# The memory stage of a two-block network rebuilt: who splits the weights, where norms, squares and products stand, and norm weights applied inside the split

## The reference, cut to what matters

```python
mem_n = rms_norm(mem, mem_norm_g)                      # 256 x 2048
h = rms_norm(x, norm_g[0])                             # 512 x 2048
proj = h @ dn_w_in                                     # decay/beta, delta net, cross attention, gates
kv = mem_n @ w_kv                                      # 256 x 2048: 4 heads, keys and values of 256
k = rms_norm(kv[..., :1024] by head, kn_g); v = kv[..., 1024:]
...                                                    # delta net (12 pairs of heads), cross attention
x = x + (concat(mix, xa) * silu(z)) @ w_out            # mix is 3072 wide, xa 1024
```

## Time and profile before

| | us |
|---|---|
| median of 3 runs | 3722.05 (3721.0 to 3726.62) |
| profiled execution | 3725.82 |
| its span | 3724.0 |
| TensorE busy in it | 3395.2 (91%) |
| VectorE, ScalarE, GpSimd busy | 1524.5, 841.8, 1786.0 |
| mean granted TensorE clock | 0.969 |

### The profile page before, as it was taken

One profiled execution on the slowest core, in us unless ns is written; L12 is line 12 of the kernel. 1 busy time (PEld: TensorE's weight loads), 2 busy tenths in 40 slices (PEclk: granted clock), 3 DMA queues, 4 the chain that ended last, 5 costly groups with the idle time before them and its releaser, 6 DMA issues.

```text
span 3724.0 us, 47370 instructions
## 1 busy us (share of the span) xinstructions
PE 3395.2 (91%) x17232; PEld 2797.9 (75%) x17232; DVE 1524.5 (41%) x2077; ACT 841.8 (23%) x1269; POOL 1786.0 (48%) x1828
## 2 busy tenths in 40 slices
PE   7699989999999999999979998999988888879897
PEld 6667777887788778877768786777767777658685
DVE  2442234444444443444342213344345555541523
ACT  4322123223322332233220101111122222210111
POOL 4545544234433443334315675666654544436574
PEclk9899999999999999999989999999999999999998
DMA  5212221111111111111124223222221112232122
GB/s 207 102 63 85 91 74 57 51 60 70 68 39 64 65 68 51 56 62 68 59 94 152 86 101 124 97 84 91 96 96 59 64 68 70 90 113 101 68 99 81
DMA packets 53364, 306.69 MB, mean 82 GB/s; under 512 B 5012, under 2 KB 7188, under 8 KB 21812
## 3 DMA queue, kind: packets, MB, share of 16 engines
q1 hardware_dynamic: 33984, 247.48, 19.1%
q10 hardware_dynamic: 19316, 58.32, 4.2%
HBM read 284.74 MB, written 21.04 MB: 82 GB/s over the span
## 4 chain that ended last, share of the span: by engine, by line
PE 73%; DVE 14%; ACT 6%; issue 5%; POOL 1%; DMA 1%; ACTq 0%; DVEq 0%; POOLq 0%; SPq 0%
PE gemm_ps L388 18%; PE gemm_ps L390 18%; PE gemm_ps L389 18%; DVE arena L774 9%; ACT arena L1417 3%; DVE arena L780 3%; PE bankC L517 3%; PE bankA L505 3%; PE bankB L515 2%; PE bankA L674 1%; POOL w_lo L346 1%; ACT L1417 1%; DVE a_lo L774 1%; PE bankB L562 1%; PE bankB L563 1%
## 5 line engine op out<-in xcount | busy, mean ns | idle before, releaser
L388 PE MATMUL gemm_ps<-a_hi,w_hi 128*128 128x512 f32 (+1 forms) x3744 | 1516.8, 405 | 116.0 <-DVE a_lo L774 83.3
L390 PE MATMUL gemm_ps<-a_hi,w_lo 128*128 128x512 f32 (+1 forms) x3744 | 1451.8, 388 | 0.0
L389 PE MATMUL gemm_ps<-a_lo,w_hi 128*128 128x512 f32 (+1 forms) x3744 | 1449.8, 387 | 0.0
L361 POOL CAST w_hi<-w_raw 128x512 fp32r<-128x512 f32 x880 | 544.6, 661 | 1825.3 <-issue 1819.3
L346 POOL TENSOR_TENSOR w_lo<-w_raw,w_hi 128x512 fp32r<-128x512 f32 x944 | 1249.5, 1354 | 70.1 <-ACT w_hi L1417 70.1
L388 PEld LDWEIGHTS gemm_ps<-a_hi,w_hi 128*128 128x128 f32 x3744 | 718.1, 192 | 283.0 <-DVE a_lo L774 72.3
L390 PEld LDWEIGHTS gemm_ps<-a_hi,w_lo 128*128 128x128 f32 x3744 | 716.3, 191 | 143.8
L389 PEld LDWEIGHTS gemm_ps<-a_lo,w_hi 128*128 128x128 f32 x3744 | 719.1, 192 | 127.8 <-issue 9.6
L774 DVE TENSOR_TENSOR arena<-gemm_ps,arena 128x512 f32<-128x512 f32 (+3 forms) x145 | 96.0, 662 | 803.2 <-PE gemm_ps L390 798.7
L774 DVE RECIPROCAL arena<-arena 128x512 f32<-128x512 f32 (+2 forms) x70 | 172.7, 2468 | 361.8 <-ACT arena L1417 359.9
L1417 ACT ACTIVATE arena<-arena 128x512 f32<-128x512 f32 (+5 forms) x334 | 204.4, 612 | 437.2 <-DVE arena L774 423.3
(11 more groups left out here) (151 smaller groups left out, 2225.5 us busy)
## 6 DMA issues: line engine op xcount, KB each, us to landing
w_raw<-w_stream SPq DMA_DIRECT2D x236, 1024.0 KB, 4.8
y_scratch<-arena ACTq DMA_DIRECT2D x20, 512.0 KB, 3.5
arena<-y_scratch ACTq DMA_DIRECT2D x15, 512.0 KB, 3.6
arena<-gc_scratch ACTq DMA_DIRECT2D x12, 512.0 KB, 3.6
arena<-x_t ACTq DMA_DIRECT2D x1, 4096.0 KB, 13.3
arena<-y_scratch ACTq DMA_DIRECT2D x1, 4096.0 KB, 25.5
x_scratch<-arena ACTq DMA_DIRECT2D x1, 4096.0 KB, 13.2
y_out<-arena ACTq DMA_DIRECT2D x4, 1024.0 KB, 3.9
```

What stands on the lines that cost most here:

```text
L361: pool.tensor_copy(part(w_hi, w, q), part(w_raw, w, q)).then_inc(pool_step, 1)
L388: pe.matmul(o, hi, a_hi[:, k, 0:width], start=(k == 0), stop=False)
L389: pe.matmul(o, hi, a_lo[:, k, 0:width], start=False, stop=False)
L390: last = pe.matmul(o, lo, a_hi[:, k, 0:width], start=False, stop=(k == KT - 1))
```

## The change

The memory stage: half of memT, the gains and the first constants come before the second weight tile and the rest, and x follows in two halves. The weight of the memory's norm is applied by ScalarE's copy into `a_hi` (its scale) and by one VectorE instruction that multiplies and subtracts into `a_lo`. Six sums of squares stand ahead of the first tile's matmuls and ten between them. VectorE makes both parts of tiles 0 and 1 and the low part of tiles 2 to 17 (one instruction of 2048 elements), ScalarE the high part of tiles 2 to 17; GpSimd starts with tile 18. Squares of x, their sums, x's root and the products of x (in place), the key norms and v's transposes stand between the tiles. Fills 4 and 7 apply the norm weight in the two parts of the split. In the last pair of heads three buffers hold y, and four blocks are split ahead of the steps. The core of the diff (cut lines of the old order are described above; engines in the order SyncE, GpSimd, TensorE, VectorE, ScalarE):

```diff
 EARLY = 6
-X_FROM = 7
+AHEAD = 4
+SELF_CUT = W_AB + 2
+X_SQUARES = {4: 0, 5: 4, 7: 8, 8: 12}
+X_PRODUCTS = {9: (0, 4), 10: (4, 8), 12: (8, 12), 14: (12, 14), 15: (14, 16)}
...
-            for w in range(2):
-                sp.dma_start(w_raw[:, w, :, :], weights[w]).then_inc(raw_loaded[w], 16)
+            sp.dma_start(w_raw[:, 0, :, :], weights[0]).then_inc(raw_loaded[0], 16)
+            sp.wait_ge(s["mem_in"], 16)
+            sp.dma_start(w_raw[:, 1, :, :], weights[1]).then_inc(raw_loaded[1], 16)
...
-            with pool.Fori(0, W_AB // 2) as i:
+            with pool.Fori(0, (W_END - SELF_CUT) // 2) as i:
                 for w in range(2):
-                    low_tile(w, i)
-            with pool.Fori(0, (W_END - W_AB) // 2) as i:
-                for w in range(2):
-                    cut_tile(w, i + W_AB // 2, i)
+                    cut_tile(w, i + SELF_CUT // 2, i)
...
+            pe.wait_ge(s["par_loaded"], 32)
+            for k in range(6):
+                memory_sum(k)
             for c in range(W_AB):
                 for k in range(KT):
                     gemm(W_MEM, c, k, 0 if c == 0 else None, width=M)
+                    if c == 0 and k + 6 < KT:
+                        memory_sum(k + 6)
+                if c % 2 == 1 and 3 <= c < 3 + 2 * XH:
+                    if c == 3:
+                        pe.wait_ge(s["root_ready"], 1)
+                    kv_sums((c - 3) // 2)
+                if c == 8:
+                    pe.wait_ge(s["x_acc"], KT)
+                    pe.matmul(bankC[:, 1, :], ones, root, start=True, stop=True).then_inc(s["sq_summed"], 1)
+                if c >= 10:
+                    if c == 14:
+                        pe.wait_ge(s["root_ready"], 2)
+                    v_transposes(c - 10)
+            for c in (6, 7):
+                v_transposes(c)
...
                 for k in range(blocks):
+                    v.wait_ge(act_hi, CUT_AT[f] + k + 1)
                     if gain is not None:
-                        for kk in ((0, 1, 2) if k == 0 else (k + 2,)):
-                            if kk < KT:
-                                product(kk)
-                    v.wait_ge(act_hi, CUT_AT[f] + k + 1)
+                        op(v.scalar_tensor_tensor, a_lo[:, k, 0:width], src[:, k, :], gains(gain + k),
+                           a_hi[:, k, 0:width].bitcast(F32), ALU.mult, ALU.subtract,
+                           sem=act_lo, value=CUT_AT[f] + k + 1)
+                        continue
                     op(v.tensor_tensor, a_lo[:, k, 0:width],
-                       stage[:, k % 4, 0:width] if gain is not None else src[:, k, :],
+                       src[:, k, :],
...
+            v.wait_ge(s["par_loaded"], 32)
+            def low_tile(t):
+                w, n = tile_at(W_MEM, t)
+                if t < 2:
+                    v.wait_ge(raw_loaded[w], 16)
+                    op(v.tensor_copy, w_hi[:, w, :, :], w_raw[:, w, :, :])
+                else:
+                    v.wait_ge(s[f"mem_hi{w}"], n)
+                op(v.tensor_tensor, w_lo[:, w, :, :], w_raw[:, w, :, :], w_hi[:, w, :, :].bitcast(F32), ALU.subtract,
+                   sem=cut[w], value=n + 1)
+            for k in range(KT):
+                v.wait_ge(act_hi, k + 1)
+                op(v.scalar_tensor_tensor, a_lo[:, k, 0:M], src_mem[:, k, :], gains(C_MEMN + k),
+                   a_hi[:, k, 0:M].bitcast(F32), ALU.mult, ALU.subtract, sem=act_lo, value=k + 1)
+                if k in (1, 9):
+                    low_tile(k // 9)
             reciprocal_root(0, M)
             for c in range(W_AB):
                 scaled(kv[:, c, :], W_MEM, c, width=M)
+                if c + 2 < SELF_CUT - 1:
+                    low_tile(c + 2)
+                if c + 2 in X_SQUARES:
+                    for k in range(X_SQUARES[c + 2], X_SQUARES[c + 2] + 4):
                         v.wait_ge(s["squared"], KT + k + 1)
                         if k == 0:
...
+                if c in KV_NORM:
+                    h = KV_NORM[c]
+                    v.wait_ge(s["kv_root"], h + 1)
+                    op(v.reciprocal, stage[:, h, 0:M], stage[:, h, 0:M])
+                    for e in range(2):
+                        op(v.scalar_tensor_tensor, kv[:, 2 * h + e, :], kv[:, 2 * h + e, :], gains(C_XK + e),
+                           stage[:, h, 0:M], ALU.mult, ALU.mult, sem=s["kv_norm"] if e else None, value=h + 1)
+                if c == 8:
+                    v.wait_ge(s["root_ready"], 2)
+                    op(v.reciprocal, root, root, sem=s["rstd_ready"], value=2)
+                if c in X_PRODUCTS:
+                    for k in range(*X_PRODUCTS[c]):
+                        op(v.scalar_tensor_tensor, src0[:, k, :], src0[:, k, :], gains(C_NORM + k), root,
+                           ALU.mult, ALU.mult, sem=s["x_made"], value=k + 1)
+            fill(1, src0, None)
+            low_tile(SELF_CUT - 1)
+            v.wait_ge(const_loaded, 16)
             copied(ab[0:64, 0, :], W_AB, 0, rows=64)
...
+            for k in range(AHEAD):
+                early_low(k)
...
+                    if made is not None:
+                        act.wait_ge(made, k + 1)
+                    op(a_hi[:, k, 0:width], src[:, k, :], ACT.Copy, act_hi, CUT_AT[f] + k + 1,
+                       scale=1.0 if gain is None else gains(gain + k))
+            half = KT // 2
+            act.dma_start(par[:, :], params).then_inc(s["par_loaded"], 16)
+            act.dma_start(src_mem[:, 0:half, :], memT[:, 0:half, :]).then_inc(s["mem_in"], 16)
+            act.dma_start(con[:, 0:4, :], consts[:, 0:4, :]).then_inc(s["par_loaded"], 16)
+            act.dma_start(src_mem[:, half:KT, :], memT[:, half:KT, :]).then_inc(s["src_loaded"], 16)
...
-            for t in range(2):
+            act.wait_ge(s["par_loaded"], 32)
+            act.wait_ge(s["mem_in"], 16)
+            for k in range(KT):
+                if k == half:
+                    act.wait_ge(s["src_loaded"], 16)
+                if k >= 2:
+                    act.wait_ge(s["sq_summed"], k - 1)
+                op(sqr[:, k % 2, 0:M], src_mem[:, k, :], ACT.Square, s["squared"], k + 1)
+                op(a_hi[:, k, 0:M], src_mem[:, k, :], ACT.Copy, act_hi, k + 1, scale=gains(C_MEMN + k))
+                if k == half + 4:
+                    act.wait_ge(act_hi, half)
+                    act.wait_ge(act_lo, half)
+                    act.dma_start(src0[:, 0:half, :], xT[:, 0:half, :]).then_inc(s["mem_in"], 16)
+            act.wait_ge(s["sq_summed"], KT)
+            op(root[:, 0:M], bankA[:, 0, 0:M], ACT.Sqrt, s["root_ready"], 1, bias=eps[:, :], scale=1.0 / D)
+            act.wait_ge(act_hi, KT)
+            act.wait_ge(act_lo, KT)
+            act.dma_start(src0[:, half:KT, :], xT[:, half:KT, :]).then_inc(s["src_loaded"], 16)
+            for t in range(2, SELF_CUT - 1):
                 high_tile(t)
+                if t == 3:
+                    act.dma_start(con[:, 4:4 + 2 * LEVELS, :], consts[:, 4:4 + 2 * LEVELS, :]).then_inc(
+                        const_loaded, 16)
+                if t % 2 == 0 and 4 <= t < 4 + 2 * XH:
+                    h = (t - 4) // 2
+                    act.wait_ge(evicted[1], h + 1)
+                    if h >= 2:
+                        act.wait_ge(s["kv_sum"], h - 1)
+                    op(kv_sqr[:, h % 2, :], kv[:, 2 * h:2 * h + 2, :].rearrange("p c m -> p (c m)"), ACT.Square,
+                       s["kv_sq"], h + 1)
+                if t % 2 == 0 and 6 <= t < 6 + 2 * XH:
+                    h = (t - 6) // 2
+                    act.wait_ge(s["kv_sum"], h + 1)
+                    op(stage[:, h, 0:M], bankA[:, h % 2, h // 2 * M:h // 2 * M + M], ACT.Sqrt, s["kv_root"], h + 1,
+                       bias=eps[:, :], scale=1.0 / (2 * P))
+                if t in X_SQUARES:
+                    act.wait_ge(s["mem_in"], 32)
+                    for k in range(X_SQUARES[t], X_SQUARES[t] + 4):
+                        if k == half:
+                            act.wait_ge(s["src_loaded"], 32)
+                        if k >= 4:
+                            act.wait_ge(s["x_acc"], k - 3)
+                        op(x_sqr[k % 4], src0[:, k, :], ACT.Square, s["squared"], KT + k + 1)
+                if t == 10:
+                    act.wait_ge(s["sq_summed"], KT + 1)
+                    op(root, bankC[:, 1, :], ACT.Sqrt, s["root_ready"], 2, bias=eps[:, :], scale=1.0 / D)
+                if t == 15:
+                    act.wait_ge(s["vT_done"], 1)
+                    op(vmem[:, :, 0:T], bankB[:, :, :], ACT.Copy, s["v_done"], 1)
+            high(1, src0, made=s["x_made"])
+            high_tile(SELF_CUT - 1)
+            act.wait_ge(s["vT_done"], 2)
+            op(vmem[:, :, T:2 * T], bankC[:, :, :], ACT.Copy, s["v_done"], 2)
...
+            def load_early(p):
+                act.dma_start(y_rows(p), y_dram[2 * p:2 * p + 2].rearrange("a p t -> p a t")).then_inc(
+                    s[f"early_y{p % 3}"], 16)
```

(14 more changed lines are left out.)

184 lines of the change are left out of this document (49 added, 135 removed).

## The result

The changed kernel takes **3635.0 us** (median of 4 runs, 3633.3 to 3638.6) against 3722.8 for the kernel before (4 runs beside it, 3721.0 to 3726.6): a ratio of 0.976, 95% interval 0.975 to 0.978. The forecast was 3636, the range 3620 to 3662. The profiled execution took 3633.3, its span is 3631.5, its mean granted clock 0.975.

What follows compares the result with a forecast made beforehand. TensorE was busy 3395 of 3724 us, the memory stage bound by a relay of ScalarE, GpSimd and TensorE; 66.9 + 6.5 + 7 + 5.5 = 85.9 us off 3722 gave 3636 us, range 3620 to 3662.

Steps and rivals of the forecast that it cites:

- One tile, the low part: Memory stage: a VectorE low part of 2048 elements takes 2.30 us; high plus low 4.3 us, hidden behind TensorE's 5.74.
- The start: Memory stage's start: ScalarE begins at 10 us, clock low until 24, tile 0 ends at 30.5 us (bounds 28 and 35.4).
- The fifteen other tiles: Memory tiles after tile 0: 86.1 us plus 6.3 for sums and transposes and 1 for the clock, ending at 123.9.
- The tail: Last memory tile to first cross-attention tile: 16.2 us instead of 44.9, x's low parts at 0.73; 66.9 us saved by 140.1.
- The gate tile and the last projection: Two later splits: blocks 0.79 us apart, low clock at first; 6.5 and 7 us saved, bounds for each 1 and 8.5.
- Four blocks ahead: w_out's first tile: four blocks go before the last head's step, three loads out; 5.5 us saved, bounds 0 and 9.
- 1 (VectorE becomes the bound): Memory stage: each tile costs 7.6 instead of 6.2 us, 21 us in 15 tiles, total 3657 us; chance 0.17.
- the 87% of the prediction: VectorE's work over the fifteen memory tiles: some 81 us of 93, making it the second bound.
- 2: Later edits give nothing: clock stays low in the splits, delayed head takes back the four blocks; 3655 us, chance 0.13.
- 3, the smaller start: Tile 0 ends at 28 and all bounds at their good ends, 3627 us; counted within the forecast's chance of 0.65.
- 4: Whole memory stage with TensorE's clock at 1.2 GHz: 10 us slower, 3732 us; chance 0.02.
- the signs that the prediction names: Profile after: among others, memory tiles 5.8 to 6.3 us apart, low part 2.3 us, blocks 0.79 us apart in both splits.

Runs made afterwards that it cites:

- experiment 2: Kernel before with only the later edits: four blocks ahead, three buffers for y, norm weights inside the splits of fills 4 and 7; 3698.5 us, ratio 0.9929.
- Experiment 7: Changed kernel with no blocks of y split ahead of the last pair's first step, three buffers and their loads kept; 3636.3 us (one run).
- experiment 4: Changed kernel with key norms and x's sixteen products moved after the last memory tile on VectorE; 3663.1 us (one run).
- experiment 5: Changed kernel with VectorE's low part of tiles 2 to 16 made twice, the result the same; 3667.3 us (one run).

## Why the prediction was right, point by point

- **One tile, the low part.** The costliest unknown was a subtraction of 2048 elements, 2.30 by the slope of two rows, the copy 1.2. VectorE in order of time, kernel after:

```profile
13.81 1.23 DVE L792 CAST w_hi<-w_raw 128x2048 fp32r<-128x2048 f32 x1
15.07 2.29 DVE L792 TENSOR_TENSOR w_lo<-w_raw,w_hi 128x2048 fp32r<-128x2048 f32 x1
```

  Both are right to 0.03 us (1.2 and 2.30 in the prediction). The figures of the Trainium skill (VectorE: DVE Perf Modes, section "The perf-mode tier table"), 1227 and 2293 ns, agree with the trace.

- **The start.** Right in the sum, with three of its steps off, and so in part by luck. ScalarE began at 11.24 and not at 10: the data had landed at 9.9, and then a table load of 1.28 us stood in the chain, which I had forgotten; the earlier trace rows hides it, since ScalarE's first work there had landed earlier than the constants. The scaled high part takes 0.51, not the 0.42 of one without a scale. On the other side the clock was low for a shorter time, until 15.4 us and not 24. The sums of squares show it. TensorE's groups, of before from 17 to 29.6 and from 30.3 to 35.8 us, then of after from 11.5 to 15.3 and from 15.8 to 28:

```profile
L397 PE MATMUL bankA<-arena,con 128*128 128x256 f32 x19 | 10.8, 718 | 19.1 <-DMA con<-shape_consts 17.4 <-ACT arena L1417 1.5
L397 PE MATMUL bankA<-arena,con 128*128 128x256 f32 x11 | 4.0, 436 | 1.9 <-ACT arena L1417 1.9
```

```profile
L398 PE MATMUL bankA<-arena,con 128*128 128x256 f32 x7 | 3.8, 708 | 11.8 <-ACT arena L1454 11.8
L398 PE MATMUL bankA<-arena,con 128*128 128x256 f32 x25 | 8.8, 431 | 0.4 <-ACT arena L1454 0.4
```

  The same instruction takes 0.72 us on average early on and 0.44 later, in both kernels. So the earlier trace rows were read rightly as the low level. The step that was off is how long it lasts: before, the sums grow short at 29.7 us, 12.3 after the first one and with pauses between; after, at 15.4, only 3.6 after the first one. The view by stretch says 1.00 for these early stretches as well, but it says so for 0 to 10 us too, in which TensorE has no work at all, and can't be used there. With the high level so early, ScalarE (1.05 us per block) was the pace of tile 0 and not TensorE, and tile 1's first matmul followed at 30.1 (30.5 predicted).

- **The fifteen other tiles.** 122.2 against 123.9: the 1 us for a fall of the clock wasn't needed, and 0.4 came from tile 0. TensorE was busy for 62.00 of 62.00 us. The two tightest loads made ScalarE wait for 5.2 and 4.7 us, at 37.5 and 44.1, and TensorE didn't feel it, as it worked on the other slot.

- **The tail.** 17.7 us and not 16.2: x's low parts stand 0.80 us apart (131.25, 132.05), not 0.73, since each takes 0.70 and some 0.1 to start. Start, tiles and tail together: 139.97 against 140.1, **66.8 us saved against 66.9**. An error of 1.7 us in one term and one of 1.5 in the next cancelled. And the 66.8 itself is that of one execution of the kernel before; experiment 2's gives 63.1, so the agreement to 0.1 us is luck.

- **The gate tile and the last projection.** 6.4 and 6.6 against 6.5 and 7. The gate tile's mechanism was not what I wrote. VectorE in order of time, kernel after:

```profile
2228.26 15.32 DVE L792 SCALAR_TENSOR_TENSOR a_lo<-arena,par,a_hi 128x512 fp32r<-128x512 f32 x16 [3.13 <-ACT a_hi L1454]
```

  Sixteen blocks take 15.32 us, 0.96 each and not 0.79. The first two, beside the end of GpSimd's cut (until 2231), take 1.65 and 1.58 us, and the other fourteen follow each other at 0.86; the granted clock was low for 6.8 us (2227.5 to 2234.3) and back at 1.00 with more than half of the blocks still to come. VectorE set the end, and TensorE's clock only the first blocks. The last projection is alike (16.92 us for the sixteen, the first four at 1.59 beside GpSimd). Two errors, the price of a block and the length of the low clock, again left the sum right.

- **Four blocks ahead.** 7.8 us against 5.5, within the bounds of 0 to 9, but by another mechanism. The step that failed is the credit: I gave the gain to the four blocks, and charged too little for the head's step that they delay. Experiment 7 shows that the blocks ahead cost 2.0 us and the third buffer with its earlier load gives 9.8.

- **The rivals.** 1 (VectorE becomes the bound) falls by experiment 4 and the releasers of the kernel after; experiment 5 shows how near it was, nearer than the 87% of the prediction says. 2 falls by experiment 2. 3, the smaller start, came true for tile 0 by 0.4 us only. 4 falls by the granted clock, 1.00 in every stretch from 20 to 207 us. Of the signs that the prediction names, two came out larger: the memory tiles with sums behind them stand 6.4 to 6.8 us apart, and the blocks in the two later splits more than 0.79.

- **What is left over.** Between 2338 and 2450 of before, 4.7 us came with no edit. There the trace of before has two falls of the clock, each behind a pause of TensorE of 2 to 3 us, that the kernel after's first profile lacks. The busy time by stretch around the second fall, of before, of after, and of after's second profile:

```profile
2418.00:2427.00 9.00, 7.14 (x21) 5.19 (x22) 7.67 (x10) 4.19 (x6) 7.40 (x7) 0.62 0.11 14
```

```profile
2335.00:2345.00 10.00, 7.28 (x38) 5.66 (x38) 8.64 (x10) 4.20 (x6) 8.54 (x8) 1.00 0.11 45
```

```profile
2338.00:2347.00 9.00, 7.35 (x22) 5.34 (x23) 7.68 (x11) 4.19 (x6) 7.20 (x6) 0.62 0.08 15
```

  The same program has the falls in one execution and not in the other. Up to the first of them its second profile is 1.3 us ahead of the first, behind the second 4.4 us late, and its span is 5.6 us longer (3637.1 and 3631.5). So these microseconds belong to the execution, not to the change. What decides it in an execution, the runs don't show.

## What to carry to other kernels

Where two buffers alternate, ask of each slot for the sum of its latencies against the time in which the consumer works on the other slot, and not only for the share that each engine is busy: a relay of 7 us on two half-idle engines cost TensorE 9 us in 62, and the same work in 4.3 us cost it none. Then ask the same of each engine, tile by tile and not on average: with a second low part VectorE's list for a tile grew to 8.4 us, longer than a tile takes TensorE, and nearly all of the 34.5 us added came through, where the slot's latency alone would have let through 6 or 7. Price an operation that is in no row by the slope of its neighbours, and ask of each row whether another engine shared the port beside it. When an edit has two parts that act on one wait (blocks ahead, and a further buffer), run each alone: here one gave 10 us and the other took 2.

## What the hardware showed that was not expected

- A scaled copy on ScalarE costs more than a plain one: 0.51 against 0.42 us for 128x256 and 0.72 against 0.63 for 128x512 (gate tile), with the scale a column in SBUF: some 0.09 us each.
- Beside GpSimd's subtractions VectorE's two-input operations take twice their time and more on average (693 to 1384 ns, 752 to 1390, 486 to 1243) and one plain copy within SBUF three times its own (0.43 to 1.44 us), while a reciprocal and an eviction from PSUM take no longer.
- TensorE left the low level 3.6 us after its first matmul in the kernel after and 12.3 us after it in the kernel before, by the length of its sums (0.71 and 0.43 us on average); a 1.00 in the view by stretch says nothing for a stretch without work. And it was granted 0.62 in 9 us of the mLSTM stage in one execution and 1.00 in another of the same program.
- ScalarE's first table load (1.28 us) starts only once the waits ahead of the first operation are met; loaded by hand before them, it gave back 1.22 us of the start.
